# A two-model layer stack on one core: heads prepared a period early, x parked in DRAM, gate projections moved last

## Time and profile before

| what | value |
|---|---|
| runs | 3487.5, 3484.78, 3488.03 us (median 3487.5) |
| the profiled execution | 3492.8 us |
| its span, first to last instruction | 3491.3 us |
| TensorE busy | 3133.2 us, 90% |
| VectorE, ScalarE, GpSimd busy | 1791.7, 887.4, 1838.4 us |
| granted TensorE clock, mean | 0.94 |
| DMA | 291.71 MB, mean 84 GB/s |

### The profile page before, as it was taken

How to read it: one execution, slowest core, us unless ns; L and a number is a source line. 1 busy time by engine, 2 the same in 40 slices (tenths; PEclk the granted TensorE clock), 3 DMA queues, 4 the chain that set the end, 5 groups by cost and what they waited for, 6 DMA issues and landing times.

```text
span 3491.3 us, 39415 instructions
## 1 busy us (share of the span) xinstructions
PE 3133.2 (90%) x15142; PEld 2426.6 (70%) x15142; DVE 1791.7 (51%) x2749; ACT 887.4 (25%) x1409; POOL 1838.4 (53%) x1860
## 2 busy tenths in 40 slices
PE   6989998869989989998698999999799999698897
PEld 4877786647867768766486777777677777477675
DVE  5456875552163569654512533332878888711413
ACT  4122213231032221233301223232333343300102
POOL 3655575415645547745075655555445555166451
PEclk8999999979999999999699999999899999799997
DMA  3223222122222222311132222222211222232121
GB/s 136 89 97 107 84 87 85 64 85 72 97 73 96 101 95 87 108 64 64 60 109 85 82 79 76 79 76 83 73 64 64 76 76 76 76 106 96 57 95 63
DMA packets 58747, 291.71 MB, mean 84 GB/s; under 512 B 5408, under 2 KB 10656, under 8 KB 28864
## 3 DMA queue, kind: packets, MB, share of 16 engines
q1 hardware_dynamic: 35520, 247.48, 20.4%
q10 hardware_dynamic: 23040, 41.71, 3.4%
HBM read 273.11 MB, written 16.06 MB: 83 GB/s over the span
## 4 chain that ended last, share of the span: by engine, by line
PE 70%; DVE 22%; ACT 6%; issue 2%; DMA 0%; DVEq 0%; ACTq 0%; POOL 0%; POOLq 0%
PE bank L336 60%; DVE rec_ex L2032 2%; DVE h_lo L1529 1%; DVE rec_small L2018 1%; PE bank L637 1%; DVE newton L1506 1%; DVE rec_cum L1989 1%; PE bank L654 1%; PE bank L646 1%; DVE newton L1508 1%; PE bank L822 1%; DVE norm_y L1562 1%; DVE last_z L2155 1%; DVE rec_weights L2069 1%; DVE rec_lq L2046 1%
## 5 line engine op out<-in xcount | busy, mean ns | idle before, releaser
L336 PE MATMUL bank<-h_hi,w_lo 128*128 128x512 f32 x3712 | 1521.8, 410 | 97.7 <-DVE h_lo L1529 72.5
L336 PE MATMUL bank<-h_lo,w_hi 128*128 128x512 f32 x3712 | 1471.6, 396 | 0.0
L336 PE MATMUL bank<-h_hi,w_hi 128*128 128x512 f32 x3712 | 1471.1, 396 | 0.0
L2209 POOL TENSOR_SCALAR w_hi<-w_raw 128x512 fp32r<-128x512 f32 x928 | 638.6, 688 | 1514.0 <-PE bank L336 1494.8
L2211 POOL TENSOR_TENSOR w_lo<-w_raw,w_hi 128x512 fp32r<-128x512 f32 x928 | 1223.0, 1318 | 77.5
L336 PEld LDWEIGHTS bank<-h_hi,w_lo 128*128 128x128 f32 x3712 | 715.3, 193 | 306.3 <-DVE h_lo L1529 78.7
L336 PEld LDWEIGHTS bank<-h_lo,w_hi 128*128 128x128 f32 x3712 | 714.8, 193 | 154.9 <-issue 13.0
L336 PEld LDWEIGHTS bank<-h_hi,w_hi 128*128 128x128 f32 x3712 | 711.9, 192 | 154.0
L864 ACT ACTIVATE raw<-bank 128x512 f32<-128x512 f32 x160 | 95.7, 598 | 389.6 <-PE bank L336 350.5
L1732 DVE SCALAR_TENSOR_TENSOR bank<-cfm_up,par,bank 128x512 f32<-128x512 f32 x232 | 175.4, 756 | 8.3
L1868 DVE TENSOR_TENSOR xT<-bank,xT 128x512 f32<-128x512 f32 x32 | 22.1, 692 | 255.3 <-PE bank L336 255.1
(11 more groups left out here) (339 smaller groups left out, 2806.2 us busy)
## 6 DMA issues: line engine op xcount, KB each, us to landing
w_raw<-in_wall SPq DMA_DIRECT2D x232, 1024.0 KB, 4.9
ssd_abc<-acs_scratch ACTq DMA_DIRECT2D x16, 512.0 KB, 3.5
h_lo<-y_scratch ACTq DMA_DIRECT2D x3, 2048.0 KB, 9.1
h_lo<-y_scratch ACTq DMA_DIRECT2D x3, 1792.0 KB, 13.3
first_xin<-in_x SPq DMA_DIRECT2D x4, 1024.0 KB, 11.5
y_scratch<-ssd_yv ACTq DMA_DIRECT2D x16, 256.0 KB, 2.2
out<-last_rows ACTq DMA_DIRECT2D x4, 1024.0 KB, 4.2
y_scratch<-cfm_uc ACTq DMA_DIRECT2D x2, 1024.0 KB, 5.2
```

The lines of the kernel that those rows point to most:

```text
L336: mm = t.matmul(bank[b][:, :], w[:, CS16[k]], h[:, k, :], start=(k == 0 and w is m.w_lo[b]), stop=(k == KT - 1 and w is m.w_hi[b] and h is ...
L2209: g.tensor_scalar(m.w_hi[b][:, part], m.w_raw[b][:, part], 1.0, 1.0, ALU.mult, ALU.mult).then_inc(*s.hi.inc(u, n))
```

## The change

1. **Units' order.** In the first block q0 and k0 come before the cz units, and head h's period holds k and v of head h+1 and q of head h+2; the attention gates az0 to az3 come last (az0 in head 2's period, az1 to az3 in head 3's), so head 3's period has three units. In the second block hg0 leaves the banded stage; periods 1 to 4 hold hg0 to hg3, periods 0, 5 and 6 only four units, and period 7 holds hg4 to hg7. Gates are applied late, to y tiles in place.
2. **Next head's queries and keys** (mean of squares, root, rotation) and the transposed values are prepared inside head h's period, on all engines; rq and rk have two buffers. Head 0's are prepared in the conformer's tail.
3. **y in SBUF, x in DRAM.** `y` is the same memory as `xT`. x is stored to DRAM in four 1 MB pieces when it is made (`keep_x`: while x is transposed at the start, and in both out products), and each piece comes back (`fetch_x`) once the low parts of that quarter of y are made. All stores and loads of y are gone, and the waits on them. ScalarE rounds y straight into `h_hi` after the last projection unit (`round_y`).
4. **w_out's first two units** now run `behind` all 16 k-tiles after the last head's `finish`, in all three stages.
5. The SSD rows of y are scaled (`scaled`) during heads 1 and 2. par1 (layer 0's parameters) is loaded at the start and layer 1's in layer 0's out product, instead of at each `norm`; par2 is loaded after x is transposed; con1 moves from ahead of x's transposes to behind them.

The core of the diff (TensorE's order, ScalarE's new helpers and last part, VectorE's attention order):

```diff
+
+
+GATES = ((), (0,), (1,), (2,), (3,), (), (), (4, 5, 6, 7))
+
+
+def att_after(l, h):
+
+    if h == 3:
+        return [("az", l, 1), ("az", l, 2), ("az", l, 3)]
+    return [("k", l, h + 1), ("v", l, h + 1), ("q", l, h + 2) if h < 2 else ("az", l, 0)]
+
+
+def band_after(i):
+    return ([(n, 2, i + 1) for n in ("bq", "bk", "bv", "bg")] if i < 7
+            else [(n, 2, 0) for n in ("hf", "hb", "hq", "hv")])
+
+
+def rec_after(j):
+
+    return ([(n, 2, j + 1) for n in ("hf", "hb", "hq", "hv")] if j < 7 else []) + [("hg", 2, g) for g in GATES[j]]
...
         names += [(n, 2, i) for n in ("bq", "bk", "bv", "bg")]
+    names += [(n, 2, 0) for n in ("hf", "hb", "hq", "hv")]
     for j in range(8):
-        names += [(n, 2, j) for n in ("hf", "hb", "hq", "hv", "hg")]
+        names += rec_after(j)
     names += [("wo", 2, j) for j in range(KT)] + [("pg", 2, j) for j in range(KT)]
     return {name: u for u, name in enumerate(names)}
...
         self.xT = big("xT", [P, KT, T])
+        self.y = self.xT
...
@@ -474,57 +495,70 @@
         for c in range(2, NT):
             unit(("a", l, c))
             unit(("g", l, c))
-        for c in range(NT):
-            unit(("cz", l, c))
         unit(("q", l, 0))
+        unit(("k", l, 0))
+        mean_of_head(l, 0, 0)
+        unit(("cz", l, 0))
+        unit(("cz", l, 1))
+        mean_of_head(l, 0, 1)
         t.wait_ge(*dve.at("uc", l, NT - 1))
         for c in range(NT):
             mm = t.matmul(bank[2][:, :], m.ones, q.uc[:, c, :], start=(c == 0), stop=(c == NT - 1))
         mm.then_inc(*pe.inc("mu", l))
-        unit(("k", l, 0))
-        unit(("v", l, 0))
+        unit(("cz", l, 2))
+        unit(("cz", l, 3), 0, 2)
+        rotate(l, 0, 0)
         t.wait_ge(*dve.at("var", l, NT - 1))
         mean_square("cfm", l)
         leave("att", l)
-        unit(("az", l, 0))
+        unit(("cz", l, 3), 1, 2)
+        rotate(l, 0, 1)
+        unit(("v", l, 0))
+        unit(("q", l, 1))
+        values_in(l, 0)
...
-            values_in(h)
-            rope(h)
-            unit(u1, 1, 2)
+            us = att_after(l, h)
+            if h == 0:
+                quarters(us, 0, 1)
             scores(h, 0)
-            unit(u2, 0, 2)
+            if h:
+                quarters(us, 0, 1)
             scores(h, 1)
+            quarters(us, 1, 2)
             turn(h, 0)
-            unit(u2, 1, 2)
+            quarters(us, 2, 3)
             values(h, 0)
             scores(h, 2)
+            quarters(us, 3, 4)
             turn(h, 1)
-            unit(u3, 0, 4)
-            unit(u3, 1, 4)
+            mean_of_head(l, h + 1, 0)
+            quarters(us, 4, 5)
             values(h, 1)
             scores(h, 3)
+            quarters(us, 5, 6)
+            mean_of_head(l, h + 1, 1)
             turn(h, 2)
-            unit(u3, 2, 4)
+            quarters(us, 6, 7)
             values(h, 2)
+            quarters(us, 7, 8)
             turn(h, 3)
-            unit(u3, 3, 4)
+            quarters(us, 8, 9)
             values(h, 3)
+            quarters(us, 9, 10)
             finish(h)
-        pair = (("wo", l, 0), ("wo", l, 1))
-        norms(3)
-        values_in(3)
-        rope(3)
+            rotate(l, h + 1, 0)
+            quarters(us, 10, 11)
+            rotate(l, h + 1, 1)
+            quarters(us, 11, 12)
+            values_in(l, h + 1)
+        us = att_after(l, 3)
         scores(3, 0)
+        quarters(us, 0, 1)
         scores(3, 1)
+        quarters(us, 1, 2)
         turn(3, 0)
-        behind(pair, ("out", l), 0, 4)
+        quarters(us, 2, 3)
         values(3, 0)
         scores(3, 2)
+        quarters(us, 3, 4)
         turn(3, 1)
-        behind(pair, ("out", l), 4, 8)
+        quarters(us, 4, 5)
         values(3, 1)
         scores(3, 3)
+        quarters(us, 5, 7)
         turn(3, 2)
-        behind(pair, ("out", l), 8, 12)
+        quarters(us, 7, 8)
         values(3, 2)
+        quarters(us, 8, 9)
         turn(3, 3)
+        quarters(us, 9, 10)
         values(3, 3)
+        quarters(us, 10, 12)
         finish(3)
-        behind(pair, ("out", l), 12, 16)
+        behind((("wo", l, 0), ("wo", l, 1)), ("out", l), 0, KT)
...
+        for j in range(8):
+            us = rec_after(j)
+            size = len(us)
             if j == 0:
-                unit(u0)
-                unit(u1)
-                far(j)
-                unit(u2, 0, 4)
-                level(j, 0)
-                values_in(j)
-                unit(u2, 1, 4)
-                level(j, 1)
-                unit(u2, 2, 4)
-                level(j, 2)
-                unit(u2, 3, 4)
+                quarters(us, 0, 6)
+            far(j)
+            if 0 < j < 7:
+                quarters(us, 0, size - 3)
+            level(j, 0)
+            values_in(j)
...
+            if j == 0:
+                quarters(us, 11, 16)
+            elif j < 7:
+                quarters(us, size + 7, 4 * size)
+            else:
+                quarters(us, 10, 13)
             combine(j)
-        pair = (("wo", 2, 0), ("wo", 2, 1))
-        far(7)
-        finish(6)
-        level(7, 0)
-        values_in(7)
-        level(7, 1)
-        level(7, 2)
-        level(7, 3)
-        behind(pair, ("out", 2), 0, 4)
-        level(7, 4)
-        level(7, 5)
-        behind(pair, ("out", 2), 4, 8)
-        level(7, 6)
-        level(7, 7)
-        behind(pair, ("out", 2), 8, 12)
-        combine(7)
+        quarters(rec_after(7), 13, 15)
         finish(7)
-        behind(pair, ("out", 2), 12, 16)
+        quarters(rec_after(7), 15, 16)
+        behind((("wo", 2, 0), ("wo", 2, 1)), ("out", 2), 0, KT)
...
+    def keep_x(stage, j):
+        if j % 4 == 3:
+            at = slice(j - 3, j + 1)
+            a.dma_start(io["xs"][at, :, :].rearrange("a p n -> p a n"), m.xT[:, at, :]).then_inc(*s.xs.inc("x", stage))
+
+    def fetch_x(stage):
+        for n in range(4):
+            at = slice(4 * n, 4 * n + 4)
+            a.wait_ge(*dve.at("h_lo", ("out", stage), 4 * n + 3))
+            a.dma_start(m.xT[:, at, :], io["xs"][at, :, :].rearrange("a p n -> p a n")).then_inc(*s.xr[n].inc(stage))
+
+    def round_y(stage, lo, hi):
         a.wait_ge(*act.now())
-        a.activation(flat(m.h_hi[:, lo:hi, :]), flat(m.h_lo[:, lo:hi, :].bitcast(F32)), ACT.Copy).then_inc(
-            *act.inc("h_hi", stage, lo))
...
                 a.wait_ge(*dve.at("sumsq", "x", n - 1))
             a.wait_ge(*act.now())
             a.activation(m.first.sq[:, :], bank[2 + n % 4][:, :], ACT.Square).then_inc(*act.inc("turned", n))
+            keep_x(0, n)
+        a.dma_start(m.con1[:, :], io["con1"]).then_inc(*s.con1.inc("con1"))
+        a.dma_start(m.par2[:, :], io["par2"]).then_inc(*s.par2.inc(2))
...
+        gate(1)
         scores(3, 3)
         turn(3, 2)
-        split_flat(stage, 12, KT - 1)
+        evac(u1, m.raw[1])
         turn(3, 3)
-        finish(3)
+        gate(2)
+        output(3)
+        evac(u2, m.raw[2])
+        stage = ("out", l)
+        round_y(stage, 0, 1)
+        round_y(stage, 1, 2)
+        gate(3)
+        rstd(q.t0[:, :], q.t1[:, :], "att", l, 3)
+        round_y(stage, 2, 4)
+        round_y(stage, 4, 8)
+        round_y(stage, 8, 12)
+        for h in range(4):
+            a.wait_ge(*dve.at("gated", l, h))
+            round_y(stage, 12 + h, 13 + h)
+        fetch_x(l)
...
+            keep_x(l + 1, j)
...
-                v.wait_ge(*s.y.at("cfm", l))
             scores(h, 0)
-            silu(q.gz[:, :], q.t0[:, :], q.t1[:, :], "az", l, h)
             scores(h, 1)
             scores(h, 2)
+            mean_of_head(l, h + 1, 0)
             scores(h, 3)
+            mean_of_head(l, h + 1, 1)
+            if h:
+                scaled(4 * h - 4)
+            unit_of_head(l, h + 1, 0)
+            unit_of_head(l, h + 1, 1)
+            mean(h)
+            rope(l, h + 1, 0)
+            rope(l, h + 1, 1)
             finish(h)
+        scores(3, 0)
+        gate(0)
+        scores(3, 1)
+        scores(3, 2)
+        gate(1)
+        scores(3, 3)
+        gate(2)
+        mean(3)
         stage = ("out", l)
...
+        low(stage, 0, m.y[:, 0, :])
+        low(stage, 1, m.y[:, 1, :])
+        low_flat(stage, 2, 4)
+        finish(3)
+        gate(3)
+        low_flat(stage, 4, 8)
         low_flat(stage, 8, 12)
-        scores(3, 3)
-        low_flat(stage, 12, KT - 1)
-        finish(3)
-        low(stage, KT - 1, q.oT[:, :])
+        for h in range(4):
+            low(stage, 12 + h, m.y[:, 12 + h, :])
```

More of the change, by code:

```diff
@@ L345, in unit, with quarters @@
         tiles(u, part * size, part * size + size)
+    def quarters(names, lo, hi):
+        for k in range(lo, hi):
+            unit(names[k // 4], k % 4, 4)
     def behind(names, stage, lo, hi):
@@ L488, in conformer, with own_bank, mean_of_head @@
         leave("att", l)
-        unit(("az", l, 0))
+        unit(("cz", l, 3), 1, 2)
[3 more added lines that the diff above has]
+        values_in(l, 0)
+    def own_bank(h):
```

(56 more changed lines are left out.)

492 lines of the change are left out of this document (228 added, 264 removed).

## The result

The changed kernel takes **3435.24 us** (median of four, 3433.46 to 3436.0), before it 3487.41; the ratio is 0.9847, 95% interval [0.9835, 0.9859]. It is 52.2 us faster, inside the range (3362 to 3438), and 41 us slower than the forecast of 3394. The profiled execution of after lies at its median.

What follows compares the result with a forecast made beforehand. TensorE, busy 90% of the span, was taken as the bound, with gains from its idle time and low clock; recurrence periods were VectorE's. First block -88.4 and recurrence -4.7 made -93.1: 3487.5 to 3394 us, range 3362 to 3438.

Steps and rivals of the forecast that it cites:

- first block, two layers: First block: TensorE's idle and slow-clock excess of 78.8 us a layer falls to 34.6, gaining 88.4 for both layers.
- up to the recurrence's first far product: Recurrence's start: half of hg0 leaves ahead of the last banded product (-5.5), its other half's evacuation leaves the fence (-5.6).
- period 0: Recurrence's first period: half a unit less of GpSimd work beside VectorE, -1.6 us.
- periods 1 to 4: Recurrence: these keep five units, one more after level 7, which fills the wait at `far`: -1 us each.
- period 7 and the handover: Recurrence's last period: four gate units cover it, w_out's pair stands behind its end; 102 us against 79.9, +22.
- the rest: Elsewhere: y's stores, parameter loads, x's traffic and the start were all priced at 0.
- The handover's three gaps: First block's handover to w_out: TensorE idles 1.7, 3.9 and 4.1 us waiting for rounding and low parts.
- Periods 5 and 6 lose a unit (3.1) and a gate (1.4): -5 each: Recurrence: VectorE-bound periods shorten by the VectorE time of the unit and gate leaving, with their waits: -5 us each.
- The recurrence loses: Rival: ScalarE's evacuations of hg4 to hg7 delay level exponentials in period 7, making it 122 us; 3414, chance 0.12.
- The recurrence gains: Rival: periods 5 and 6 at 66 us and period 7 at 90, 24 better; 3370, chance 0.12.
- VectorE becomes the bound: Rival, first-block heads: VectorE slowed beside GpSimd, heads idle 8 instead of 2.5, handover costs 5 more; 3437, chance 0.17.
- x's traffic starves the weights: Rival, three out products and handovers: 24 pieces of 1 MB push weight loads back, 118 us; 3512, chance 0.03.

Runs made afterwards that it cites:

- the handover's experiment: Kernel after with rounding and low parts put ahead of the last head's tanh, root, finish and gate at the handovers to w_out (in the recurrence only partly): 3414.0 us.
- ScalarE's order alone: Kernel after with ScalarE's query-unit evacuation and tanh moved behind the next head's logarithms and gathering copies in periods 0, 5 and 6; TensorE untouched: 3412.1 us.
- all units earlier: Kernel after with TensorE's quarters moved so that units in periods 5 and 6, and period 0's query unit, end sooner against the levels: 3405.6 us.

## Why the forecast was 41 us off

By the spans, term by term, the periods from far product to far product (minus is faster):

| term | predicted | measured |
|---|---|---|
| first block, two layers | -88.4 | -85.7 |
| up to the recurrence's first far product | -11.1 | -14.6 |
| period 0 | -1.6 | +8.0 |
| periods 1 to 4 | -4 | -1.4 |
| periods 5 and 6 | -10 | +15.6 |
| period 7 and the handover | +22 | +22.7 |
| the rest | 0 | -2.3 |
| sum | -93.1 | -57.6 |

- **First block: right.** Per layer 43.6 and 42.0 against 44.2. Its parts: the mean in the conformer's tail waits 6.1 (said 6.2), the variance 3.9 (1.7), the first scores 3.6 (2.5; what ends last there is ScalarE's copy of the transposed values, which itself waits for VectorE's conformer gate), a middle head's idle time is 1.7 or 1.4 (2.5), head 3's 2.5 (1.0). The handover's three gaps are 2.1, 3.9 and 2.6 in layer 0 and 2.1, 2.4 and 2.4 in layer 1 (1.7, 3.9, 4.1), and the handover's experiment showed that this order was worth 21 us. The earlier trace rows did not stretch the heads: VectorE is busy 35.9 of 47.5 us.
- **Period 7: right**, 102.7 against 102, though the terms that I listed for it add up to 103.1. VectorE's gathering ends 54.8 us after the far product (54 said), and the gaps at the pair are 3.0 and 3.4 (2.8, 4.6 and 1.2).
- **Periods 0, 5 and 6: wrong, 35 us.** The step that failed is "Periods 5 and 6 lose a unit (3.1) and a gate (1.4): -5 each", with period 0's -1.6. It priced the work that leaves a period and took the places of what stays as given. The runs showed 23 us (ScalarE's order alone) to 30 us (all units earlier) of the 35 to be order: the units of a four-unit period ended a place later against the levels, and ScalarE, which evacuates them in its written order, held VectorE's exponentials and logarithms. The diff said so in the argument of `quarters`; I did not set each unit's last quarter against ScalarE's list. With the order mended (all units earlier) the two periods take 72.9 and 73.4 from far product to far product, on average 3.0 under before's 76.2 where 5 was said: the term was also 2 us too large. Part of that is the gate: head 3's is still applied in period 5 (the row of 59.29 above has it), so of the two only period 6 loses one. The other period that loses a gate is period 1, and it is the one of periods 1 to 4 that got shorter, 74.9 against 79.1.
- **The rivals.** "The recurrence loses" named this mechanism, for period 7 and 20 us; it was in periods 0, 5 and 6. Period 7 was free of it. "The recurrence gains" was counted as 24 us where its own windows make 22. "VectorE becomes the bound" gave 3437 and is wrong all the same: its heads would idle 8 us each, and they idle under 3. That its number is the nearest to 3435 says nothing for it. "x's traffic starves the weights" is closed by the run without it, "the recurrence gains" by periods 5 and 6. That the time fell inside the range at all is owed to its upper end, which was set for these rivals and not for the step that failed.
- **The medians.** 5.3 us of the 41 are the profiled execution of before, whose excess over its median I did not account for.

What is still open: periods 2 and 4 of after, with five units as before, take 77.4 and 77.5 us where they took 76.4 and 75.8, and no run here shows why.

## What to carry to other kernels

When work leaves a period, don't only price what leaves: list, for each unit that stays, after which step it now ends, and what stands behind its evacuation in the order of the engine that evacuates it. An engine that is busy 30% can set the time by its order alone. Price a handover with the order of each engine written beside it; what doesn't need the last result goes first.
